# Loading the third and fourth expert of a mixture-of-experts layer by three transfers of 4 MB each

## What is computed

```python
logits = x2 @ w_router + b_router
top_vals, top_idx = lax.top_k(logits, TOP_K)          # 4 of 32
gates = jax.nn.softmax(top_vals)
# for every expert e, over the tokens routed to it:
h = x2[tok] @ w_gu[e] + b_gu[e]                       # 1024 x 2048 weights, 8 MB
g = jnp.minimum(h[:, :D_FF], 7.0); u = jnp.clip(h[:, D_FF:], -7.0, 7.0)
y = (u + 1.0) * (g * jax.nn.sigmoid(1.702 * g))
out = y @ w_down[e] + b_down[e]                       # 1024 x 1024 weights, 4 MB
```

## Time and profile before

| | us |
|---|---|
| median of 3 runs | 1148.26 |
| the profiled execution, whole | 1146.75 |
| its span, which all rows below are counted in | 1144.8 |
| outside the span (1146.75 less 1144.8) | 1.95 |
| PE busy in the span | 1059.2 (93%) |
| DVE, ACT, POOL busy | 442.3, 153.9, 59.9 |
| bytes moved | 444.87 MB, 389 GB/s over the span |

### The profile page before, as it was taken

How to read it: one execution, slowest core, us unless ns; L and a number is a source line. 1 busy time by engine, 2 the same in 40 slices (tenths; PEclk the granted TensorE clock), 3 DMA queues, 4 the chain that set the end, 5 groups by cost and what they waited for, 6 DMA issues and landing times.

```text
span 1144.8 us, 20191 instructions
## 1 busy us (share of the span) xinstructions
PE 1059.2 (93%) x8037; PEld 465.0 (41%) x8039; DVE 442.3 (39%) x1311; ACT 153.9 (13%) x334; POOL 59.9 (5%) x38
## 2 busy tenths in 40 slices
PE   9999999998999669999976669999979989999997
PEld 8876559543333213333321213333323333343333
DVE  2767577572533213333321113333313323333324
ACT  2142111230111001111100001111101101111101
POOL 0503370000000000000000000000000000000000
PEclk9999999999999889999987879999999999999999
DMA  9965356989999999999999999999999999999996
GB/s 331 365 233 184 110 189 253 379 324 428 423 433 428 437 430 432 432 429 434 428 437 430 432 433 428 434 428 437 429 433 434 427 433 426 436 428 429 433 425 248
DMA packets 36105, 444.87 MB, mean 389 GB/s; under 512 B 3876, under 2 KB 5160, under 8 KB 21256
## 3 DMA queue, kind: packets, MB, share of 16 engines
q1 hardware_dynamic: 33320, 439.86, 91.2%
q10 hardware_dynamic: 2752, 4.54, 1.3%
HBM read 443.34 MB, written 1.05 MB: 388 GB/s over the span
## 4 chain that ended last, share of the span: by engine, by line
PE 70%; DMA 23%; DVE 3%; another core or an unknown queue 2%; ACT 1%; issue 1%; DVEq 0%; SPq 0%; POOL 0%; POOLq 0%
PE bank L1005 23%; DMA ring<-in_w_down 15%; PE bank L1030 13%; DMA ring<-in_w_gu 8%; PE bank L689 6%; PE bank L981 6%; PE bank L635 5%; PE bank L968 3%; PE bank L814 2%; PE bank L877 2%; PE bank L974 2%; PE bank L1012 1%; PE bank L1018 1%; PE bank L1023 1%; PE bank L999 1%
## 5 line engine op out<-in xcount | busy, mean ns | idle before, releaser
L1005 PE MATMUL bank<-ring,wk 128*32 128x512 f32 x3072 | 369.9, 632 | 63.4 <-DMA ring<-in_w_gu 63.3
L1005 PEld LDWEIGHTS bank<-ring,wk 128*32 128x32 f32 x3072 | 103.9, 116 | 302.4 <-issue 263.8
L1030 PE MATMUL bank<-ring,wk 128*32 128x512 f32 x1632 | 204.8, 600 | 6.2 <-DMA ring<-in_w_down 6.2
L2036 DVE TENSOR_SCALAR wk<-bank 128x256 f32<-128x256 f32 x51 | 21.6, 423 | 461.3 <-PE bank L1005 460.5
L981 PE MATMUL bank<-wk 64*128 64x512 f32 x416 | 103.3, 615 | 2.9 <-ACT wk L1436 2.9
L1030 PEld LDWEIGHTS bank<-ring,wk 128*32 128x32 f32 x1632 | 62.8, 110 | 74.7 <-issue 46.8
L1424 ACT ACTIVATE wk<-wk 128x256 f32<-128x256 f32 x51 | 21.2, 417 | 455.0 <-DVE wk L2036 455.0
L635 PE MATMUL bank<-ring 128*128 128x256 f32 x320 | 70.7, 381 | 0.0
L689 PE MATMUL bank<-ring 128*128 128x512 f32 x152 | 66.4, 593 | 0.0
L981 PEld LDWEIGHTS bank<-wk 64*128 64x128 f32 x416 | 35.8, 186 | 71.4 <-issue 64.0
L635 PEld LDWEIGHTS bank<-ring 128*128 128x128 f32 x320 | 60.2, 190 | 8.9 <-issue 0.8
(11 more groups left out here) (369 smaller groups left out, 881.4 us busy)
## 6 DMA issues: line engine op xcount, KB each, us to landing
ring<-in_w_gu SPq DMA_DIRECT2D x55, 4096.0 KB, 34.8
ring<-in_w_down SPq DMA_DIRECT2D x27, 4096.0 KB, 38.4
ring<-in_w_gu SPq DMA_DIRECT2D x18, 2048.0 KB, 13.4
ring<-in_w_down SPq DMA_DIRECT2D x9, 2048.0 KB, 11.8
ring<-in_w_in SPq DMA_DIRECT2D x4, 2048.0 KB, 19.3
ring<-in_w_ck SPq DMA_DIRECT2D x2, 2048.0 KB, 21.7
ring<-in_w_cv SPq DMA_DIRECT2D x2, 2048.0 KB, 18.0
ring<-in_w_cq SPq DMA_DIRECT2D x2, 2048.0 KB, 8.3
```

What stands on the lines that cost most here:

```text
L1005: ins = mm(hidden(bank, g), rows[:, kk, c, :], half_columns(w[:, kk, :], g), start=False, stop=2 * c + kk == KT - 1, skip_group_check=True)
L1030: ins = mm(strip(7, 2 * d + b), actT[:, b, 2 * c + gg, :], wd[:, gg, b, 512 * d:512 * d + 512], start=c == 0 and gg == 0 and b == 1, stop= ...
```

## The change

The third and fourth expert are each loaded by three transfers of 4 MB (`load_unit`) in place of six of 2 MB. Each transfer waits until both slots of its unit are back, as `load_later` does for every later expert. `load_in_pieces` goes. As these loads don't raise the even slots' `slot_landed` any more, PE's waits count one less: `loads` is 1 from the third expert on, and 2 in the last expert's even chunks. What PE computes and the order of its instructions stay as they are, and so do the ring and everything on the other engines.

```diff
-            def load_in_pieces(e, u, i, used):
-                at = UNIT_SLOT[u * UNITS_PER_EXPERT + i]
-                src = w_gu[bass.ds(e, 1), i].rearrange("o p n -> (o p) n") if i < 2 else w_down[bass.ds(e, 1)].rearrange("o p n -> (o p) n")
-                for h in range(2):
-                    sp.wait_ge(chunk_used[2 * i + h], used)
-                    sp.nop(nofuse=True)
-                    landed = unit_landed[u * UNITS_PER_EXPERT + i] if h else slot_landed[at]
-                    sp.dma_start(slot_words(at + h), src[:, h * SLOT:h * SLOT + SLOT]).then_inc(landed, 16)
-
...
             for i in range(UNITS_PER_EXPERT):
-                load_in_pieces(third, 0, i, used_by_first)
+                sp.wait_ge(chunk_used[2 * i], used_by_first)
+                sp.wait_ge(chunk_used[2 * i + 1], used_by_first)
+                sp.nop(nofuse=True)
+                load_unit(third, 0, i)
...
             for i in range(UNITS_PER_EXPERT):
-                load_in_pieces(fourth, 1, i, used_by_second)
+                sp.wait_ge(chunk_used[2 * i], used_by_second)
+                sp.wait_ge(chunk_used[2 * i + 1], used_by_second)
+                sp.nop(nofuse=True)
+                load_unit(fourth, 1, i)
...
                         if c % 2 == 0:
-                            pe.wait_ge(slot_landed[s], 16 * (front_loads[s] + 3))
+                            pe.wait_ge(slot_landed[s], 16 * (front_loads[s] + 2))
...
-                    expert_pass(it, u, 2, ending)
+                    expert_pass(it, u, 1, ending)
...
-                        two_passes(heavy_turn, u, 2)
+                        two_passes(heavy_turn, u, 1)
```

## The result

The changed kernel takes 1150.66 us in the median of 20 runs (1148.73 to 1154.27), the kernel before 1148.26 us (20 runs). The ratio is 1.0021 with a 95% interval of 1.0015 to 1.0028: 2.4 us slower (1.7 to 3.2). The predicted time was 1148.6 us, within a range of 1147.3 to 1151.2. The range holds the measured time, but only because it was drawn wide enough for the second rival, which had the size; the likeliest case, +0.3 us, was not what happened. By its mechanism the forecast was wrong, and that the time lies in the range is luck.

What follows compares the result with a forecast made beforehand. The prediction took the unbroken DMA stream to bound the kernel. A 0.4 us gain from larger transfers and about 0.7 us of dry queue at the fourth's `w_down` made +0.3 us: 1148.26 + 0.3 = 1148.6 us, range 1147.3 to 1151.2.

Steps and rivals of the forecast that it cites:

- The rule for a thin cover: Any joined 4 MB transfer: lands no earlier than its issue plus 12.2 us, nor than the landing ahead plus 9.71.
- A: Third expert's unit 0, first thin place: joined issue at 251.27 in place of 249.56, cover 4.4 falling to 2.7 us.
- C: Fourth expert's w_down (unit 2), last thin place: joined issue at 300.75 in place of 298.46, cover 1.8 us, the thinnest.
- holes in the early engines are free: DMA stream at the thin covers: only the latest of 16 engines, which sets the landing, has to be hit.
- Unit 0 of the third: Third expert's first joined transfer: 263.5 by issue against 263.7 by queue, so the queue decides and nothing is lost.
- Unit 0 of the fourth: Fourth expert's first joined transfer: cover 2.9 us, 292.4 by issue against 292.8 by queue, nothing lost.
- `w_down` of the fourth: Fourth expert's unit 2: lands at 312.95 for 312.65, queue dry about 0.7 us, +0.3 us with the gain included.
- The gain of larger packets: Whole changed stream: twelve times 4.89 us become six times 9.71, a gain of 0.4 us if the queue never runs dry.
- Rival 2: Fourth expert's w_down: a thin cover costs more than the lone transfer says, +2.1 to +3.0 us; chance 0.20.
- Rival 3: Whole stream: every transfer carries a fixed cost and six fewer save it, at most 15 us, 1133 us; chance 0.01.
- Rival 1: Thin covers: the queue doesn't run dry for the latest engine, leaving only the gain, -0.4 us, 1147.9 us; chance 0.12.
- A later cover: Stream behind the changed transfers: a later transfer issued with a cover under 3 us would make the prediction wrong altogether.

Runs made afterwards that it cites:

- a_later: Kernel before, the third expert's first four pieces held until the first expert's chunk 3 is used: 1.0030 (1.0018 to 1.0041), +3.4 us.
- c_later: Kernel before, the two pieces of the fourth expert's w_down held until the third expert's chunk 1 is used: 1.0041 (1.0028 to 1.0054), +4.7 us.
- again: The changed kernel once more, with a second trace, against the kernel before: 1.0016 (1.0005 to 1.0027), +1.8 us.
- after: First trace of the changed kernel, all six units joined, against the kernel before: 1150.66 us, 1.0021 (1.0015 to 1.0028).
- a_joined: Kernel before with only unit 0 of the third expert joined, the other five units in pieces: 1.0005 (0.9995 to 1.0014).
- c_joined: Kernel before with only the fourth expert's w_down joined: 1.0011 (1.0002 to 1.0020), +1.3 us.
- ac_joined: Kernel before with unit 0 of the third expert and the fourth's w_down joined, four units in pieces: 1.0005 (0.9996 to 1.0015), +0.6 us.
- late_pieces: Kernel before with its twelve 2 MB transfers, each piece waiting until both slots of its unit are back: 1.0015 (1.0006 to 1.0025), +1.7 us.
- best_again: Second run of the kernel before with m_joined's joins and the first piece at A and C cut into two 1 MB halves: 0.9998 (0.9989 to 1.0007).
- m_joined: Kernel before with only units 1 and 2 of the third expert and unit 1 of the fourth joined: 0.9998 (0.9989 to 1.0008).

## Why the prediction was right or wrong

**What bounds the kernel** held: a_later and c_later show delays of the stream at full price at the end, and in the changed kernel the last landing is 3.8 us later after the zero, and so is the end of the span.

**The issue times** held but for the shift of the front. 252.29, 281.24 and 302.17 less 1.02 are 251.27, 280.22 and 301.15, for 251.27, 280.23 and 300.75. The 0.4 us at the last I can't explain; it is the same in again and in none of the others with the dip.

**The rule for a thin cover**, a landing no earlier than the issue plus 12.2, held too where it decided: 12.6 and 12.1 at A in after and again, 12.2 in a_joined, 12.4 at C in c_joined. At C the changed kernel took 12.7 (again) and 13.8 (after), and the pieces of a_later and c_later 13.3 to 13.5. So 12.2 is a lower bound and not the time. How the 2.5 us around the bytes were divided was wrong as well: the prediction put 1.3 to 1.6 us behind the last byte. At A in the changed kernel the last engine's end packet stands 1.0 us ahead of the landing, and the rest is in the first packets, which are slow (last section).

**The step that failed** is the sentence that holes in the early engines are free. The 279 GB/s in the microsecond from 300 were misread as well: not many engines waited there. By the packets' own times at least 90% of the 16 engines had one in flight in each quarter of it; eleven packets of 16 KB that start between 299.8 and 301.0 took 0.87 to 1.67 us instead of 0.61. The bytes were missing all the same (C's 0.59), and I took them for free, because I took the latest engine as the clock of the stream. In the kernel before it stood some 2 us behind the middle engine, so a wait of the others seemed to fit in its shadow. And it did, for one landing. By the end packets of unit 0 of the third expert the last engine is 2.3 and 2.4 us behind the middle one in the two traces before, and 0.6 and 0.2 us in after and again: the middle one stands 1.7 us later, the last one doesn't. But the stream goes on, some engine is held up again, and a landing needs all 16. At the next landing the last engine of after and again is 1.5 and 1.6 us behind the middle one once more, and now behind a later field. So the first trace's second landing comes 10.6 us after the one before, with a cover of 9.2.

```profile
q1 hardware_dynamic: 69, 2.13, 99.2%
q8 instruction: 1, 0.02, 1.2%
```

**The sum, term by term.** Unit 0 of the third: predicted 0, measured 1.6 us of hole more than before. Unit 0 of the fourth: predicted 0, measured 0.3. `w_down` of the fourth: +0.7 us of hole predicted, about 0.3 more than before measured, as the first two had moved the stream back and so given it cover. The cover at A, too, was less than the 2.7 us predicted: 1.4 and 2.1 us in after and again, as the landing ahead varies. The gain of larger packets, 0.4 us for all six, is too small to be seen here. Sum: +0.3 predicted, +2.3 by the holes, +2.4 by the timed runs.

**Rival 2** had the size (+2.1 to +3.0 us) and the remark that it decides when covers fall to 3 us. Its place was wrong by the count of holes: it put the loss on the last of the three, and two thirds arose at the first. Its remark that the losses don't add up held between A and C (a_joined, ac_joined), but not so far that only one counts. Alone, A took +0.6 us (-0.6 to +1.6) and C +1.3 us (+0.2 to +2.3): by time neither makes up the whole, and neither place can be ranked above the other. **Rival 3**, a fixed cost for each transfer in the stream, is out: late_pieces has twelve transfers and again six, with the same time. The 2.0 us that the prediction takes from the Trainium skill ("DMA: Bandwidth & Descriptors", the anatomy of one DMA) is fitted there on transfers issued from GpSimd; these go out from SP. **Rival 1** is out by the result.

**A later cover** was one of my marks for being wrong, and came near: in the changed kernel the transfer issued at 1003.10 had 4.0 us of cover, and its step was 10.7 us, 1.0 more than 9.71. Its landing:

```profile
ring<-in_w_down SPq DMA_DIRECT2D x1, 4096.0 KB, 14.7
```

In the kernel before the transfer at that place had 5.5 us and lost nothing. But again had 3.7 us of cover there (issue at 1002.12), and its step was 9.7: the landing lost nothing. So no limit for a cover can be read from landings; 4 us can already be thin.

## What to carry to other kernels

A landing is the time of the slowest of 16 DMA engines plus its acknowledgement. In a stream that bounds the kernel, the question for a later issue is when most engines run dry, which can be 2 us ahead of the landing. Here is the count for A. The middle engine ends the transfer ahead at 17.1 us after the zero (17.0 to 17.2 in all traces but best_again), and 1.0 us passes from an issue to its first byte on an empty queue, so the issue is needed by 16.1. The first piece went out at 16.0, the joined transfer at 17.7, 1.6 us too late, and 1.6 us is what the hole grew by.

Read that from the packets or from the DMA share in short stretches, not from the landings, which can stay where they are while most engines lose time. A stretch must be longer than a packet takes (1.2 us for 32 KB), or a full stream shows rows of 0.00 as well. Two transfers in place of one cost this full queue nothing that the runs could resolve, and they buy an earlier issue. Joining was free where the cover stayed above 5 us (m_joined); nothing was tested between that and the three thin places.

## What was not expected of the hardware

The landing at A didn't show the loss in any of the five traces with the late issue (29.8 to 30.3 us after the zero, for 28.8 to 30.5 in the six with the first piece in its old place) while the engines together lost 1.6 us more there.

The first packets after an empty queue are slow. In the changed kernel the 16 first ones from 253.27 us on took 12.1 us more than full speed together, 0.76 each; at the 2 MB pieces of a_later and c_later it was 0.51 and 0.58 each. Beside the 1.0 us from issue to first byte (252.29 to 253.27) this is part of what a dry queue costs.

Traces of kernels that differ only in how SP loads have or lack a dip of PE's clock, 3.4 us at 1.2 GHz in place of 2.4 from about 261 us on. It goes with a release of slots 1.7 us later, 40 us behind it (C out at 67.2 and 65.5 us), and so with the price of a thin cover. Whether it comes and goes from one execution of a program to the next, and makes part of the spread of these runs (1148.73 to 1154.27 us), was not tested.
